# Hybrid decoder layer, first attention: values as the stationary operand in column halves, heads of a long and a short row tile in turn, transposes three units behind the scores

## The chip, the cores and the metric

The kernel runs on one core of a Trainium2 chip. A core has TensorE (PE; its weight loads, PEld, are recorded apart), VectorE (DVE), ScalarE (ACT), GpSimd (POOL) and SyncE (SP), which issues DMAs. Matrix products go to PSUM (eight banks of 128 partitions x 512 float32), everything else lives in SBUF. The metric is device time of one launch in microseconds (us), lower is better, as the median of several runs.

## What is computed

One layer on 512 tokens, width 1024. A combined projection feeds two causal attentions of eight heads each, whose gated outputs pass one output projection and a LayerNorm with a residual. The first attention (branch A) is the one that the change touches: each query attends to the 128 keys that an indexer ranks highest. Cut to what matters:

```python
h = x @ w_in[l]
(qa, ka, va, ga, iq, ik, iw, c_q, c_kv, k_rope, gb) = _split_cols(h)
# branch A, per block of 128 queries
score = jnp.einsum('bth,bths->bts', iwb, jax.nn.relu(logits))
_, sel = lax.top_k(score, k_top)
att = jnp.einsum('bthd,btkhd->bhtk', qb, ks) * scale
p = jax.nn.softmax(att, axis=-1)
o = jnp.einsum('bhtk,btkhd->bthd', p, vs)
o_a = _dsa_branch(qa, ka, va, iq, ik, iw) * jax.nn.silu(ga)
o_b = _mla_branch(...) * jax.nn.silu(gb)
out = jnp.concatenate([o_a, o_b], axis=-1) @ w_out[l]
x = _layernorm(DEEPNORM_ALPHA * x + out, ln_g[l], ln_b[l])
```

## The kernel before

Every engine has its own hand-written instruction list; semaphores join them. Up to 166 us the projections run, each product split into high and low parts (`products`, L1117), and beside them the indexer: its logits (`idx_logits`, L1221) use four groups of 32 array rows at once. VectorE finds the top keys and leaves a bias per query and key (`spans`), so that the selection becomes a mask over all keys up to the row.

The two attentions are one loop over **units** `u`, a head of a row tile of 128 queries: 0 to 31 are attention A (`NU_A` = 32), 32 to 63 attention B (`NU` = 64). `ORDER = [3, 2, 1, 0]` says which row tile comes first: heads of the tile with 512 keys, then 384, 256, 128. N is the number of keys of a unit. In step `u` of the loop the engines do:

- TensorE: `scores(u)` (A: L1308 and L1311, the high and low parts of queries and keys; B: L1318, float32) into one of two banks `ps_s`, free when the mask of u - 2 is done; `transposes(u - 2)` (L1353, `T_LAG` = 2), the N/128 tiles of the probabilities into one of two banks `ps_pT`, free when their copy is done; `outputs(u - 4)` (A: L1369, B: L1384, `PV_LAG` = 4). For A the stationary operand is a 128 x 128 tile of the transposed probabilities, streamed are the 64 columns of the head's values; the result has queries as partitions.
- VectorE: `mask_unit(u)` (L944) adds the mask into `probs` (four buffers) and takes the row maximum. For A, per row tile, `normalise` (L960, L961) and `apply_gate` (L970); for B `probs_low` (L975, the low part of the transposed probabilities), `read_pair` (L990) and others. In steps 3 to 6 it also does `qpe_blocks` (L932), a part of B's queries.
- ScalarE: `copy_probsT(u - 2)` (L704) from the bank to `probsT` (three buffers), then `exp_unit(u)` (L684), whose sum per row goes to `row_sum`; the high parts of B's values, `vb_high` (L728), at `VB_EARLY` = 20, 32 and 33.
- GpSimd: splits the output weights into high and low parts (L515, L519), then two of the four low parts of B's values (L522), then the second half of the weights' low parts (L528), then the merging of B's head pairs (L332) and the scaling of B's gate (`scale_gate`, L504).

The gated rows of A are turned by `o_transposes(i, 0)` (L1398): the first row tile at step `O_FIRST + T_LAG` = 18, the others during B. The products with the output weights, `out_products` (L1425), fill TensorE during B: the first half of the first row tile from step `A_HALF_AT` = 34, two matmuls a step, the rest from step 49.

## Time and profile before

| | |
|---|---|
| median of 3 runs | 301.89 us (301.46 to 301.92) |
| profiled execution | 301.67 us, span 299.9 us |
| TensorE busy | 291.2 us (97%) |
| TensorE weight loads | 248.6 us (83%) |
| VectorE busy | 228.5 us (76%) |
| ScalarE busy | 165.6 us (55%) |
| GpSimd busy | 169.8 us (57%) |
| first mask of A to first score of B | 166.4 to 208.0 us |
| granted TensorE clock | 1.00 of full speed (2.4 GHz) in every stretch up to 290 us |

Busy time is the union of an engine's recorded instructions. A record runs from an instruction's start to its end and overlaps with the next one's, so what an instruction costs an engine that is full is the distance from start to start; the chain of waits gives this directly. The difference of about 1.8 us between the execution's time and its span lies around the span.

### The profile page before, as it was taken

The numbers are of one execution on the slowest core, as the hardware profiler recorded it, in microseconds if no ns is written. First come the engines' busy times: TensorE is split into PE (matmuls) and PEld (weight loads), VectorE is DVE, ScalarE is ACT, GpSimd is POOL, SyncE is SP. The second block draws the span as 40 slices with busy tenths as digits, with TensorE's granted clock in tenths as the row PEclk, the third lists the DMA queues.
The fourth block names the chain that finished last, engine by engine and source line by source line (L and its number), as shares of the span: only waits on it lengthen the run. The fifth ranks groups of instructions, "written<-read, shape, count | busy, mean of one in ns | idle before, by whom it ended". The sixth has DMA issues, their size and how long they took to land.

```text
span 299.9 us, 5192 instructions
## 1 busy us (share of the span) xinstructions
PE 291.2 (97%) x1664; PEld 248.6 (83%) x1664; DVE 228.5 (76%) x523; ACT 165.6 (55%) x397; POOL 169.8 (57%) x197
## 2 busy tenths in 40 slices
PE   8999999999999999999999999999999999999990
PEld 7999987778888888888888789998677788888890
DVE  2898689879999999994134663564898878977785
ACT  4754533692252272383267787888877786553200
POOL 5798965106999975445317697630594161817211
PEclk9999999999999999999999999999999999999996
DMA  7965552200533723220056577301940000030412
GB/s 230 354 183 179 144 149 75 67 0 0 154 96 102 207 76 105 70 72 0 0 149 143 211 203 156 125 2 43 359 161 3 0 0 2 36 106 3 140 70 72
DMA packets 19547, 31.86 MB, mean 106 GB/s; under 512 B 6496, under 2 KB 9056, under 8 KB 19520
## 3 DMA queue, kind: packets, MB, share of 16 engines
q1 hardware_dynamic: 19088, 31.35, 34.4%
q8 instruction: 14, 0.23, 0.3%
q10 hardware_dynamic: 432, 0.18, 0.3%
q14 instruction: 13, 0.11, 0.1%
HBM read 26.28 MB, written 2.10 MB: 95 GB/s over the span
## 4 chain that ended last, share of the span: by engine, by line
PE 93%; DVE 2%; DMA 1%; ACT 1%; issue 1%; DVEq 0%; ACTq 0%
PE ps L1117 50%; PE ps L1425 15%; PE ps L1353 6%; PE ps L1318 5%; PE ps L1369 5%; PE ps L1384 3%; PE ps L1308 2%; PE ps L1132 2%; PE ps L1311 2%; PE ps L1221 1%; DMA w_raw<-in_w_in 1%; PE ps L1242 1%; PE ps L1398 1%; DVE y_last L1031 0%; ACT probs L684 0%
## 5 line engine op out<-in xcount | busy, mean ns | idle before, releaser
L474 POOL TENSOR_TENSOR w_lo<-w_raw,w_hi 128x512 fp32r<-128x512 f32 (+3 forms) x62 | 79.3, 1301 | 34.0 <-ACT w_hi L573 33.8
L1117 PE MATMUL ps<-w_hi,x_lo 128*128 128x512 f32 (+2 forms) x224 | 82.6, 372 | 0.0
L1117 PE MATMUL ps<-w_lo,x_hi 128*128 128x512 f32 (+2 forms) x224 | 82.5, 371 | 0.0
L573 ACT ACTIVATE w_hi<-w_raw 128x512 fp32r<-128x512 f32 (+3 forms) x62 | 35.9, 590 | 68.9 <-PE ps L1117 61.8
L1117 PE MATMUL ps<-w_hi,x_hi 128*128 128x512 f32 (+1 forms) x188 | 73.6, 391 | 0.0
L1117 PEld LDWEIGHTS ps<-w_hi,x_lo 128*128 128x128 f32 x224 | 42.1, 188 | 6.5
L1117 PEld LDWEIGHTS ps<-w_lo,x_hi 128*128 128x128 f32 x224 | 42.2, 188 | 6.0
L1425 PE MATMUL ps<-wo_hi,oT 128*128 128x512 f32 (+1 forms) x144 | 43.5, 372 | 0.0
L1117 PEld LDWEIGHTS ps<-w_hi,x_hi 128*128 128x128 f32 x188 | 35.3, 188 | 7.1 <-ACT w_hi L573 0.7
L684 ACT ACTIVATE probs<-probs,small 128x512 f32<-128x512 f32 (+3 forms) x64 | 35.8, 559 | 7.6 <-DVE small L944 7.0
L1353 PE MATMUL ps<-ident,probs 128*128 128x128 f32 x160 | 28.3, 274 | 0.4 <-ACT probs L684 0.2
L1425 PEld LDWEIGHTS ps<-wo_hi,oT 128*128 128x128 f32 x144 | 25.7, 189 | 3.3
L1353 PEld LDWEIGHTS ps<-ident,probs 128*128 128x128 f32 x160 | 20.1, 140 | 9.5 <-issue 5.2
L332 POOL TENSOR_TENSOR obT<-half_sum,crossed 64x128 f32<-64x128 f32 x30 | 15.7, 522 | 17.8 <-ACT crossed L737 16.1
L901 DVE MATCH_REPLACE8 score<-small,score 128x256 f32<-128x256 f32 (+2 forms) x48 | 25.7, 554 | 0.0
L944 DVE CUSTOM_DVE_ANT_0 probs<-ps,score 128x512 f32<-128x512 f32 (+2 forms) x24 | 13.3, 556 | 15.1 <-PE ps L1311 15.1
L898 DVE MAX8 small<-score 128x8 f32<-128x256 f32 (+2 forms) x48 | 23.7, 556 | 0.0
L944 DVE CUSTOM_DVE_ANT_0 probs<-ps,causal 128x128 f32<-128x128 f32 (+3 forms) x40 | 17.8, 444 | 7.0 <-PE ps L1318 3.4
L1318 PE MATMUL ps<-kbT,qbT 96*128 96x512 f32 (+3 forms) x64 | 22.7, 435 | 0.0
L1369 PE MATMUL ps<-va,probsT 128*128 128x64 f32 x160 | 21.4, 264 | 0.0
L1369 PEld LDWEIGHTS ps<-va,probsT 128*128 128x128 f32 x160 | 20.5, 193 | 0.6 <-issue 0.6
L975 DVE TENSOR_TENSOR probsT_b<-ps,probsT_b 128x512 fp32r<-128x512 f32 (+3 forms) x32 | 15.6, 488 | 5.0 <-ACT probsT_b L704 4.7
(164 smaller groups left out, 548.5 us busy)
## 6 DMA issues: line engine op xcount, KB each, us to landing
w_raw<-in_w_in SPq DMA_DIRECT2D x20, 512.0 KB, 3.7
...
```

Of the source, the lines that this page charges most:

```text
L332: eng.tensor_tensor(obT[rows, g % 4], half_sum[rows, g % 2, a], crossed[rows, g % 2], ALU.add).then_inc(pair_merged, 1)
L474: pool.tensor_tensor(w_lo[:, s, 0:n], w_raw[:, s, 0:n], w_hi[:, s, 0:n], ALU.subtract).then_inc(w_lo_ready, 1)
L573: act.activation(dst, w_raw[:, s, 0:n], ACT.Copy).then_inc(w_hi_ready, 1)
L684: act.activation(probs[:, u % NPROBS, 0:N], probs[:, u % NPROBS, 0:N], ACT.Exp, bias=neg_max[:, u % 8:u % 8 + 1], scale=-1.0, accum_out=ro ...
L898: step(V.max(top8[:, 8 * j:8 * j + 8], sc))
L901: step(V.match_replace(out=sc, in_to_replace=top8[:, 8 * j:8 * j + 8], in_values=sc, imm_value=TAKEN))
L944: V.tensor_tensor_reduce(out=probs[:, u % NPROBS, 0:N], in0=ps_s[:, u % 2, 0:N], in1=bias, scale=-scale, scalar=3.0e38, op0=ALU.add, op1=A ...
L1117: ins = mm(dst, a, b, start=start and j == 0, stop=stop and j == len(pairs) - 1)
L1318: ins = mm(ps_s[:, b, 0:N], qbT[:, h, t], kbT[:, h, 0:N], start=True, stop=True)
L1353: ins = nc.tensor.transpose(bank[:, j * P:(j + 1) * P], probs[:, u % NPROBS, j * P:(j + 1) * P], ident[:, :])
L1369: ins = mm(ps_o[:, v % 2, h * A_DIM:(h + 1) * A_DIM], probsT[:, u % 3, j * P:(j + 1) * P], va[:, j, h * A_DIM:(h + 1) * A_DIM], start=(j = ...
L1425: ins = mm(out_ps(i, b), oT[i % 2][:, o, k, :], w[:, wcols], start=first, stop=final)
```

## The change

Attention A's loop is written anew; B's arithmetic stays.

- **Order.** Units 0 to 15 take heads of the tiles with 512 and 128 keys in turn, units 16 to 31 those of 384 and 256 (`BLOCKS`). `row_sum` has its columns by rank (`sum_col`).
- **Lags.** Transposes of A come three steps behind the scores (`A_T_LAG`), outputs five (`A_PV_LAG`), for four units at once (`u % 4 == 3`).
- **Outputs** (new L1465). The head's 64 value columns are stationary, 128 columns of the transposed probabilities stream. Of two heads of one row tile the first writes partitions 0 to 63, the second 64 to 127 of the same bank columns, and their matmuls alternate. The result is already turned (head dimension as partitions). Each of the four row tiles has its own bank (`oa_bank`), two of them the banks of the output products.
- **Copies.** VectorE copies three of four transposed units of A, ScalarE the fourth (`by_dve`, `ACT_COPY`), into nine buffers (`buffer_of`, `copy_free`).
- **Gate.** Division and gate move: `row_sums_a` (reciprocals on VectorE, after all units of a block), `scale_gate_a` (GpSimd multiplies the gate's rows), `o_transposes(v, 0)` turns the scaled gate instead of the gated rows, at steps 28, 36, 38, 30 (`TURN_AT`), `turn_gate` (ScalarE) copies it to SBUF, `gate_oaT` (VectorE) multiplies it with the outputs, a step later. `copy_oT_hi` and `oT_low` read the product there; for the first row tile the latter is on GpSimd.
- **Around it.** `VB_EARLY` is 22, the first half of the output products starts at step 41 with three matmuls a step, and GpSimd does its last two weight splits between its first merges.

The diff, cut to its core:

```diff
+    BLOCKS = [(0, 3), (1, 2)]
+    A_RANK = [v for block in BLOCKS for v in block]
+    BLOCK_UNITS = 2 * HEADS
     def unit(u):
-        v, h = divmod(u, HEADS)
+        if u < NU_A:
+            n, r = divmod(u, BLOCK_UNITS)
+            v, h = BLOCKS[n][r % 2], r // 2
+        else:
+            v, h = divmod(u, HEADS)
         m = ORDER[v % TT]
         return v, m, h, (m + 1) * P
 
-    O_AFTER = [[NU_A + HEADS * (i + 1) + OT_AT - T_LAG + b for b in range(2)] for i in range(TT - 1)] + [[NU, NU]]
-    O_AFTER[0][0] = O_FIRST
+    def turned_at(u):
+        return [w for w in (u - A_T_LAG, u - T_LAG) if 0 <= w < NU and (w < NU_A) == (w == u - A_T_LAG)]
+    def buffer_of(u):
+        r = u % BLOCK_UNITS % 7
+        return r if r < 5 else r + 2 * (u // BLOCK_UNITS)
+    def last_user(u):
+        return max([w for w in range(u) if buffer_of(w) == buffer_of(u)], default=None)
+    def sum_col(u):
+        v, m, h, N = unit(u)
+        return HEADS * (A_RANK.index(v) if v < TT else v) + h
+    O_AFTER = [[turned_at(TURN_AT[i])[-1], NU_A + HEADS * (i + 1) + OT_AT - T_LAG + 1 if i < TT - 1 else NU] for i in range(TT)]
...
-    probsT = sb("probsT", 26, [P, 3, BANK])
+    probsT = [sb(f"probsT{j}", kib, [P, BANK]) for j, kib in enumerate((24, 26, 28, 30, 92, 88, 90, 94, 96))]
...
+        def by_dve(u):
+            return u < NU_A and u % 4 != ACT_COPY
+        def wait_copied(eng, u):
+            n = sum(by_dve(w) for w in range(u + 1))
+            if by_dve(u):
+                eng.wait_ge(probsT_copied_dve, n)
+            else:
+                eng.wait_ge(probsT_copied, u + 1 - n)
+        def copy_free(eng, u):
+            if u < NU_A:
+                if last_user(u) is not None:
+                    eng.wait_ge(pv_done, 4 * (last_user(u) // 4 + 1))
+                elif buffer_of(u) >= 7:
+                    eng.wait_ge(qpe_placed, 16 * P // SQ)
+                return probsT[buffer_of(u)][:, 0:unit(u)[3]]
+            if u >= NU_A + 3:
+                eng.wait_ge(pv_done, u - 2)
+            return probsT_b[:, u % 3, 0, 0:unit(u)[3]]
+        def oaT(i):
+            return gate[:, ORDER[i], 0:A_WIDTH].rearrange("p (a b) -> p a b", a=4)
+        def oa_bank(v):
+            return (ps_o, ps_y)[A_RANK.index(v) // 2][:, A_RANK.index(v) % 2]
...
-            for j in (3, 2):
+            def scale_gate_a(v):
+                m = ORDER[v]
+                pool.wait_ge(rinv_a_ready, A_RANK.index(v) // 2 + 1)
+                wait_tok(pool, G_GA, m)
+                g3 = gate[:, m, 0:A_WIDTH].rearrange("p (h d) -> p h d", h=HEADS)
+                r = rinv_a[:, HEADS * (A_RANK.index(v) % 2):HEADS * (A_RANK.index(v) % 2 + 1)]
+                pool.tensor_tensor(g3, g3, r.unsqueeze(2).broadcast_to([P, HEADS, A_DIM]), ALU.mult).then_inc(gate_a_scaled, 1)
+            def vb_low_pool(j):
                 pool.wait_ge(vb_hi_ready, VB_ORDER.index(j) + 1)
                 pool.tensor_tensor(vb_parts[j][:, :, 1:3], vb[:, j, :].rearrange("p (q a d) -> p q a d", a=2, d=V_DIM),
                                    vb_parts[j][:, :, 0:4:3], ALU.subtract).then_inc(vb_lo_pool, 1)
-            for j in range(KT, 2 * KT):
-                k = j // 2
+            def wo_low_b(k):
                 pool.wait_ge(raw_b_loaded[k - KT // 2], 16)
                 pool.wait_ge(wo_hi_ready, 2 * WO_ORDER.index(k) + 2)
-                pool.tensor_tensor(wo_lo(k, j % 2), wo_raw_b[:, k - KT // 2, j % 2], wo_hi[:, k, j % 2],
-                                   ALU.subtract).then_inc(w_lo_ready, 1)
+                for h in range(2):
+                    pool.tensor_tensor(wo_lo(k, h), wo_raw_b[:, k - KT // 2, h], wo_hi[:, k, h],
+                                       ALU.subtract).then_inc(w_lo_ready, 1)
+            for v in BLOCKS[0]:
+                scale_gate_a(v)
+            vb_low_pool(3)
+            oT_low(pool, 0, 0)
+            vb_low_pool(2)
+            for v in BLOCKS[1]:
+                scale_gate_a(v)
+            for k in range(KT // 2, KT - 2):
+                wo_low_b(k)
...
+                if g <= 2:
+                    wo_low_b(KT - 3 + g)
...
-                if u >= 3:
-                    act.wait_ge(pv_done, u - 2)
-                dst = probsT[:, u % 3, 0:N] if u < NU_A else probsT_b[:, u % 3, 0, 0:N]
+                dst = copy_free(act, u)
...
+            def turn_gate(v):
+                n = slot_of[v, 0]
+                act.wait_ge(transposed, n + 1)
+                act.activation(gate[:, ORDER[v], 0:A_WIDTH], ps_pT[:, n % 2], ACT.Copy).then_inc(gate_a_turned, 1)
...
+                if n == 0:
+                    act.wait_ge(pv_done, BLOCK_UNITS)
...
-            def normalise(v):
-                dve.wait_ge(pv_done, HEADS * (v + 1))
-                after(V.reciprocal(rinv, row_sum[:, HEADS * v:HEADS * (v + 1)]))
-                V.tensor_tensor(o_norm[:, :].rearrange("p (h d) -> p h d", h=HEADS),
-                                ps_o[:, v % 2].rearrange("p (h d) -> p h d", h=HEADS),
-                                rinv.unsqueeze(2).broadcast_to([P, HEADS, A_DIM]), ALU.mult).then_inc(o_ps_read, 1)
-            def apply_gate(v):
-                m = ORDER[v % TT]
-                cols = slice(A_WIDTH * (v // TT), A_WIDTH * (v // TT + 1))
-                dve.wait_ge(o_ps_read, v + 1)
-                wait_tok(dve, G_GA, m)
-                V.tensor_tensor(gate[:, m, cols], o_norm[:, :], gate[:, m, cols], ALU.mult).then_inc(o_ready, 1)
+            def copy_probsT(u):
+                dve.wait_ge(transposed, slot_of[u] + 1)
+                V.tensor_copy(copy_free(dve, u), ps_pT[:, slot_of[u] % 2, 0:unit(u)[3]]).then_inc(probsT_copied_dve, 1)
+            def row_sums_a(n):
+                dve.wait_ge(probs_ready, BLOCK_UNITS * (n + 1))
+                if n > 0:
+                    dve.wait_ge(gate_a_scaled, 2 * n)
+                V.reciprocal(rinv_a, row_sum[:, BLOCK_UNITS * n:BLOCK_UNITS * (n + 1)]).then_inc(rinv_a_ready, 1)
+            def gate_oaT(v):
+                half = gate[:, ORDER[v], 0:A_WIDTH]
+                dve.wait_ge(gate_a_turned, A_RANK.index(v) + 1)
+                dve.wait_ge(pv_done, BLOCK_UNITS * (A_RANK.index(v) // 2 + 1))
+                V.tensor_tensor(half, oa_bank(v), half, ALU.mult).then_inc(o_ps_read, 1)
...
-                if 0 < v <= TT and j == PV_LAG and v != TT - 1:
-                    normalise(v - 1)
-                if 0 < v <= TT and j == PV_LAG + 1 and v != TT - 1:
-                    apply_gate(v - 1)
-                if u == NU_A:
-                    normalise(TT - 2)
-                if u == NU_A + 2:
-                    apply_gate(TT - 2)
+                if u in (BLOCK_UNITS + 2, NU_A + 2):
+                    row_sums_a(u // BLOCK_UNITS - 1)
+                if u - 1 in TURN_AT:
+                    gate_oaT(TURN_AT.index(u - 1))
                 if v > TT and j == 2:
                     row_sums(v - 1)
                 if PET_AT <= u < PET_AT + TT:
                     qpe_blocks(u - PET_AT)
-                if u == O_FIRST + T_LAG + 1:
-                    oT_low(V, 0, 0)
...
-                    if h == 0:
-                        if v < 2:
-                            pe.wait_ge(acc_read[v], ACC_LAST[v])
-                        else:
-                            pe.wait_ge(o_ps_read, v - 1)
-                        if v == 0:
-                            for t in range(TT):
-                                wait_tok(pe, G_V, t)
-                    pe.wait_ge(probsT_copied, u + 1)
-                    for j in range(m + 1):
-                        ins = mm(ps_o[:, v % 2, h * A_DIM:(h + 1) * A_DIM], probsT[:, u % 3, j * P:(j + 1) * P],
-                                 va[:, j, h * A_DIM:(h + 1) * A_DIM], start=(j == 0), stop=(j == m))
-                    ins.then_inc(pv_done, 1)
+                    if u % 4 < 3:
+                        return
+                    if u % BLOCK_UNITS == 3:
+                        for b in range(2):
+                            bank = 2 * (u // BLOCK_UNITS) + b
+                            pe.wait_ge(acc_read[bank], ACC_LAST[bank])
+                        for t in range(TT):
+                            wait_tok(pe, G_V, t)
+                    for w in (u - 3, u - 2):
+                        v, m, h, N = unit(w)
+                        for a in range(2):
+                            wait_copied(pe, w + 2 * a)
+                        for j in range(m + 1):
+                            for a in range(2):
+                                ins = mm(oa_bank(v)[A_DIM * a:A_DIM * (a + 1), h // 2 * P:(h // 2 + 1) * P],
+                                         va[:, j, (h + a) * A_DIM:(h + a + 1) * A_DIM],
+                                         probsT[buffer_of(w + 2 * a)][:, j * P:(j + 1) * P], start=(j == 0), stop=(j == m))
+                                if j == m:
+                                    ins.then_inc(pv_done, 1)
...
-                            pe.wait_ge(acc_read[2 + b], ACC_LAST[2 + b])
+                            pe.wait_ge(o_ps_read, 3 + b)
...
-                if 0 <= u - T_LAG < NU:
-                    transposes(u - T_LAG)
-                if u - PV_LAG >= 0:
+                for w in turned_at(u):
+                    transposes(w)
+                if 0 <= u - A_PV_LAG < NU_A:
+                    outputs(u - A_PV_LAG)
+                if u - PV_LAG >= NU_A:
                     outputs(u - PV_LAG)
                 i, j = divmod(u - NU_A, HEADS)
-                if u == O_FIRST + T_LAG:
-                    o_transposes(0, 0)
-                if 0 < i < TT and OT_AT <= j < OT_AT + 2 and (i > 1 or j > OT_AT):
-                    o_transposes(i - 1, j - OT_AT)
-                if 0 <= u - A_HALF_AT < 12:
-                    out_products(0, 2 * (u - A_HALF_AT), 2 * (u - A_HALF_AT + 1))
+                for t in range(TT):
+                    if u == TURN_AT[t]:
+                        o_transposes(t, 0)
+                if 0 < i < TT and j == OT_AT + 1:
+                    o_transposes(i - 1, 1)
+                if 0 <= u - A_HALF_AT < 8:
+                    out_products(0, 3 * (u - A_HALF_AT), 3 * (u - A_HALF_AT + 1))
...
-O_FIRST = 16
-A_HALF_AT = 34
+O_FIRST = 33
+TURN_AT = [28, 36, 38, 30]
+A_T_LAG, A_PV_LAG = 3, 5
+ACT_COPY = 3
+VB_EARLY = 22
+A_HALF_AT = 41
```

TensorE, steady stretch of attention A. Before, the heads of the 512-key tile; L1308 and L1311 are scores, L1353 transposes, L1369 outputs:

```order
L1308 MATMUL ps<-kaT,qaT 128x512
L1311 MATMUL ps<-kaT_swap,qaT 128x512
L1353 MATMUL ps<-ident,probs 128x128 x4
L1369 MATMUL ps<-va,probsT 128x64 x4
L1308 MATMUL ps<-kaT,qaT 128x512
```

After, one step with outputs and its neighbours; L1399 and L1402 are the scores, L1444 the transposes, L1465 the outputs (the numbers in probsT_105 and so on tell the nine buffers apart):

```order
L1399 MATMUL ps<-kaT,qaT 128x512
L1402 MATMUL ps<-kaT_swap,qaT 128x512
L1444 MATMUL ps<-ident,probs 128x128
L1465 MATMUL ps<-probsT_105,va 64x128
L1465 MATMUL ps<-probsT_107,va 64x128
...
L1465 MATMUL ps<-probsT_106,va 64x128
L1465 MATMUL ps<-probsT_101,va 64x128
L1399 MATMUL ps<-kaT,qaT 128x128
L1402 MATMUL ps<-kaT_swap,qaT 128x128
L1444 MATMUL ps<-ident,probs 128x128 x4
```

The four output matmuls that stood in every step now stand as ten (three more pairs of the first two are left out) in every fourth, with streamed and stationary operand exchanged, and a long score is followed by a short transpose.

VectorE, steps 19 and 20 of attention A, with the semaphores that each row waits for. Before, masks (L944) and little else:

```order
L944 ISA probs,small<-ps,score 128x256 [waits transposed,scores_ready]
L944 ISA small 128x1
L342 TENSOR_TENSOR oT_68<-ps,oT_68 128x512 [waits oT_hi_ready]
L944 ISA probs,small<-ps,score 128x256 [waits transposed,scores_ready]
L944 ISA small 128x1
```

After, from mask 19 on (L1034) with the copies (L1049) of units 16 and 17:

```order
L1034 ISA probs,small<-ps,score 128x256 [waits transposed,scores_ready]
L1034 ISA small 128x1
L1049 COPY probsT_101<-ps 128x384 [waits pv_done,transposed]
L1034 ISA probs,small<-ps,score 128x384 [waits transposed,scores_ready]
L1034 ISA small 128x1
L1049 COPY probsT_102<-ps 128x256 [waits pv_done,transposed]
```

A copy now stands between most masks, and it waits for outputs (`pv_done`) as well as for its transposes.

TensorE, first steps of attention B (L1318, new L1409, are its scores). Before, at step 35, the output products (L1425) fill each step:

```order
L1318 MATMUL ps<-kbT,qbT 128x512
L1353 MATMUL ps<-ident,probs 128x128 x4
L1369 MATMUL ps<-va,probsT 128x64
L1425 MATMUL ps<-wo_hi,oT_68 128x512
L1425 MATMUL ps<-wo_lo_a,oT_68 128x512
```

After, steps 33 to 36:

```order
L1409 MATMUL ps<-kbT,qbT 128x512
L1444 MATMUL ps<-ident,probs 128x128 x3
L1409 MATMUL ps<-kbT,qbT 128x512
L1444 MATMUL ps<-ident,probs 128x128 x6
L1409 MATMUL ps<-kbT,qbT 128x512
L1444 MATMUL ps<-ident,probs 128x128 x4
```

The products are gone from these steps and come from step 41 on.

## Rows read from the trace of the kernel before

**Rows 1.** The page: busy time and share by engine; the chain of waits by engine.

```profile
PE 291.2 (97%) x1664; PEld 248.6 (83%) x1664; DVE 228.5 (76%) x523; ACT 165.6 (55%) x397; POOL 169.8 (57%) x197
...
PE 93%; DVE 2%; DMA 1%; ACT 1%; issue 1%; DVEq 0%; ACTq 0%
```

**Rows 2.** Windows: stretch, length, busy us (records) of PE, PEld, DVE, ACT, POOL, clock.

```profile
172.20:208.00 35.80, 35.56 (x296) 33.83 (x294) 19.22 (x71) 29.72 (x92) 21.01 (x25) 1.00 0.38 102
```

**Rows 3.** The chain of waits in attention A: start, length, what.

```profile
177.01 0.84 PE ps L1369 x8
177.85 0.29 PE ps L1308
178.13 0.23 PE ps L1311
178.37 0.44 PE ps L1353 x4
```

**Rows 4.** Waits, 165 to 240 us: us in total, times, longest.

```profile
DVE probs L944 <- PE ps L1311: 18.4, 25, 2.5
```

**Rows 5.** A's output matmuls: ns min/median/max, first and last start.

```profile
L1369 PE MATMUL ps<-va,probsT x160: 219/275/275, 175.1 to 213.8; 128*128 128x64 f32 x160
```

**Rows 6.** The chain: scores of B with 128 streamed float32 columns.

```profile
254.12 0.22 PE ps L1318 x2
```

**Rows 7.** Timeline of PE around the indexer's logits: start, length, line, shapes, count.

```profile
48.47 0.39 PE L1117 MATMUL ps<-w_hi,x_lo 128*128 128x512 f32 x1
48.79 0.45 PE L1221 MATMUL ps<-ik_hi,iq_hi 32*128 32x384 f32 x4
49.07 0.35 PE L1221 MATMUL ps<-ik_lo,iq_hi 32*128 32x384 f32 x4
49.24 0.35 PE L1221 MATMUL ps<-ik_hi,iq_lo 32*128 32x384 f32 x4
49.52 0.50 PE L1117 MATMUL ps<-w_hi,x_hi 128*128 128x512 f32 x1
49.85 0.39 PE L1117 MATMUL ps<-w_lo,x_hi 128*128 128x512 f32 x1
```

**Rows 8.** The chain: scores behind transposes; two products with output weights.

```profile
173.11 0.23 PE ps L1308
...
212.06 0.52 PE ps L1425 x2
```

**Rows 9.** Timeline of DVE: masks, copies, a small transpose [idle before <-releaser].

```profile
167.01 0.69 DVE L944 CUSTOM_DVE_ANT_0 probs<-ps,score 128x512 f32<-128x512 f32 x1
167.62 0.08 DVE L944 DVE_READ_ACCUMULATOR2_ANT small<- 128x1 f32 x1
167.74 2.52 DVE L952 COPY kbT<-ps 64x512 f32<-64x512 f32 x4
...
174.22 0.44 DVE L932 STREAM_TRANSPOSE qpe_blk<-qpe_tok 128x256 f32<-128x256 f32 x1
174.59 0.65 DVE L944 CUSTOM_DVE_ANT_0 probs<-ps,score 128x512 f32<-128x512 f32 x1
...
202.72 0.29 DVE L944 CUSTOM_DVE_ANT_0 probs<-ps,causal 128x128 f32<-128x128 f32 x1 [0.45 <-PE ps L1311]
202.94 0.08 DVE L944 DVE_READ_ACCUMULATOR2_ANT small<- 128x1 f32 x1
```

**Rows 10.** Timeline of ACT: a copy and an exponential of 512 columns.

```profile
174.34 0.59 ACT L704 ACTIVATE probsT<-ps 128x512 f32<-128x512 f32 x1
174.82 0.72 ACT L684 ACTIVATE probs<-probs,small 128x512 f32<-128x512 f32 x1
...
175.53 0.59 ACT L704 ACTIVATE probsT<-ps 128x512 f32<-128x512 f32 x1
```

**Rows 11.** Timeline of POOL: last weight split; a gate's scaling.

```profile
193.71 2.51 POOL L519 TENSOR_TENSOR wo_lo_a<-w_raw,wo_hi 128x512 fp32r<-128x512 f32 x2
...
230.01 1.05 POOL L504 TENSOR_TENSOR gate<-gate,small 128x512 f32<-128x512 f32 x1 [0.88 <-POOL obT L332]
```

42 lines of the change are left out of this document (23 added, 19 removed).

## The prediction

> **What bounds the kernel now.** I read the busy shares and the chain of waits first: TensorE is busy for 97% of the span and stands for 93% of the chain [rows 1]. Then the stretches: in the first attention (172.2 to 208) TensorE is busy 35.56 of 35.80 us while VectorE is busy 19.22 and ScalarE 29.72 [rows 2]. So what counts is TensorE's work in a row, unless the change makes it wait. Next, what one unit (a head of a row tile) costs there: pieces of the chain are start to start, so they add up. A long unit (512 keys) takes 0.29 + 0.23 us for its two score matmuls, 0.44 for four transposes and 0.84 for probabilities times values: eight recorded matmuls, two for each of four key chunks [rows 3]. So a chunk costs 0.21 us, though only 64 columns stream. The last part is the largest of the unit, and VectorE waits for it in the end: 18.4 us of its idle time before the masks is waiting for scores [rows 4].
>
> **Values stationary.** All 160 recorded matmuls of this step [rows 5] change form. In the old form each loads 128 stationary columns and streams 64. In the new one each loads 64 and streams 128, and two heads' matmuls write different halves of the output partitions, in alternation. Two bounds. If the halves run one after the other, a chunk costs what a float32 matmul with 128 streamed columns costs here: 0.22 us for the pair of records [rows 6], no gain on 0.21. If they run side by side, two heads' chunks take that time together, 0.105 to 0.11 each: 80 chunks x 0.105 = 8.4 us saved. Which of the two? The nearest row is the indexer, with four row groups: twelve matmuls of 384 columns stand in three groups of four with one start each, 0.17 us from the second group to the third, which is the time of one such matmul [rows 7]. TensorE thus runs disjoint parts of the array side by side, by rows; by columns no row shows it, nor for float32. I take side by side, -8.4, and keep 0 as the other end.
>
> The Trainium skill, TensorEngine Tiling (Array Packing), section Key Properties, says that different tiles load and multiply in parallel and that changing the tiling mode drains the engine. By its first half the gain is the -8.4 just given; its second half speaks against this change, and by it the eight groups of outputs below must pay something. The indexer's row agrees with both halves, for row tiles.
>
> **Changes of array form.** The outputs now come in eight groups of four units, each entered from and left to full-array matmuls. The indexer's excursion has the same price tag: the last full matmul starts at 48.47 and streams 0.23; the first one after it starts at 49.52 and is followed only 0.33 later instead of 0.23. That is 0.82 + 0.10 us, of which 3 x 0.17 is work: 0.41 over [rows 7]. It contains the exposed first load of four tiles. The least is none, if the halves switch freely. I take 0.35, nearer to the row: 8 x 0.35 = +2.8 (0 to 3.3).
>
> **Scores behind transposes.** A long score pair costs 0.52 right behind an output step but its first matmul only 0.23 behind transposes [rows 3, 8]. Before, nearly every unit stood behind outputs; now one in four. About ten long units gain 0.06: -0.6.
>
> **VectorE copies three of four transposed tiles.** Its own pace, start to start: mask of 512 columns 0.61, copy of 512 columns 0.61 (four in 2.52), mask of 128 columns 0.22 [rows 9]. I price the copy of 128 at 0.22 too. A pair (long and short) costs VectorE 0.61 + 0.22 for masks, 0.61 for the long copy and 0.11 for half the short ones: 1.55 us. TensorE needs for the pair 0.46 + 0.23 for scores, 0.55 for transposes, 5 x 0.105 for outputs and 0.18 for the switch: 1.95. ScalarE has two exponentials, 0.71 for the one of 512 columns and less for the one of 128, and a short copy every second pair, where even a 512-wide one costs it 0.48 [rows 10]: at most 1.7. So in the steady stretch TensorE still bounds, with VectorE at 80%; it would have to lose 0.4 us per pair before it takes over.
>
> At the start there is no such cover. Outputs begin only at unit step 8 (before: 4), and score 8 needs mask 6. Until then VectorE has masks 2 to 6 (3 x 0.61 + 2 x 0.22), copies 0 to 2 (1.44) and three of its four small transposes for the queries at 0.37 [rows 9]: 4.8 us, starting half a us behind TensorE. TensorE has scores 2 to 7 and transposes 0 to 4: 2.07 + 1.54 = 3.6 us. It waits 5.3 - 3.6 = about +1.8 (0.8 to 2.3).
>
> **Added waits.** First, the copy of unit 16 (VectorE, step 19) goes into a buffer last read by unit 14, whose outputs TensorE issues only in step 20. Behind that copy stand mask 20 and copy 17; transposes 18 need the bank that copy 16 frees, scores 22 need mask 20. After the outputs TensorE has only 0.23 us of scores before it meets the 0.48 of the copy, then again at mask 20: +0.5 (0.2 to 1.0). Second, at steps 33 to 35 VectorE has the two low parts of the values (512 columns, 0.61 each like the copy) between copy 30 and mask 34; ScalarE's third high part waits for them, and its copies of 31 and 32 queue behind that: TensorE waits about +0.5 for a bank (0 to 1.5). This stretch used to be covered by products with the output weights (0.52 the pair in [rows 8]); these now start at step 41 instead of 34. The 24 of them are the same work, so their move costs only what it uncovers.
>
> **Gates.** The gate's half is turned by TensorE four times, as the attended rows were before: 4 x 0.44 in both. Division and gating drop two 512-wide VectorE operations per row tile to one; VectorE isn't the bound, so 0. The scaling goes to GpSimd (four at 1.05), behind its weight splits, which end at 193.71 + 2.51 = 196.2 [rows 11]. TensorE turns the first gate at step 28. By the prices above the outputs of step 8 end at about 172.2 + 7.5, and each four steps after them take 3.9: step 28 ends near 199.5; GpSimd has the gate at 196.2 + 1.05 = 197.3. No cost, with 2 us of slack. No queue of DMAs is reordered; the later loads of the output weights still wait for the scores of unit 31, which come no later.
>
> **Sum** against the profiled execution's 301.67 us (span 299.9; the median of the runs is 301.89): -8.4 + 2.8 - 0.6 + 1.8 + 0.5 + 0.5 = -3.4. That is 298.3 on that execution and 298.5 on the median.
>
> **Rivals.** (a) The column halves do not run side by side. For it: no row shows column halves, and in this kernel a float32 matmul is two passes on the same tile in a row, which leaves only the second pass of one head to meet the first of the other. Against it: the indexer's groups. Then 0 replaces -8.4, and VectorE's lateness at the start remains: +2.8 + 1.8 + 0.5 - 0.6 (the waits at 16 partly vanish), 306.4. The gain is used up once a chunk costs 0.105 + 3.4 / 80 = 0.15 us; above that the kernel is slower than before. (b) The halves overlap, but VectorE sets the pace: its copies and masks queue for scores and banks so that each pair costs 0.2 more, 16 x 0.2 = +3.2, 301.7, no change. For it: VectorE would be at 80%, and its masks have slack of just two score banks. Against it: a copy needs no answer from TensorE before the next mask. (c) The switches are nearly free and waits are short: -8.4 + 0.5 - 0.6 + 1.8 + 0.5 = -6.2, 295.7. For it: the exposed part of the indexer's excursion belongs to four loads of 128 columns, here it would be two of 64. (d) The gate or the values' low parts come late from GpSimd at steps 28 to 36: +1.5 on the forecast, 300.0.
>
> **How the numbers follow.** Forecast 0.50, (c) 0.13, (d) 0.07: faster, 0.70. (b) 0.10: half of it within 0.2%, since a measurement of this kernel can tell about 0.2% (0.6 us) from no change; the rest splits evenly. (a) 0.20: slower. That makes faster 0.71, same 0.06, slower 0.23. The likeliest case alone, with the ends of its terms, runs from 296.0 to 301.0. The range for 8 in 10 adds most of (c) and all of (b) and (d), and of (a) the part in which the switches or waits are cheap: 295.0 to 304.5.
>
> **What would show it.** Right: in the new profile the output matmuls (128 streamed, 64 stationary columns) stand in the chain at about 0.42 us per group of eight records, 1.05 us for a group of four units; VectorE busy rises to nearly 30 us in the stretch of the first attention; TensorE has a gap of 1 to 2 us in its first 6 us, and another near the 20th unit; the first score of the second attention comes about 4 us earlier than 207.97. Wrong: eight records at 0.84 or more (a); a chain that runs through VectorE's copies in the steady stretch (b); full matmuls right behind the outputs without a delay (c); the gate's transposes waiting for GpSimd (d).

## The result and the profile after

| | before | changed |
|---|---|---|
| median, first set of runs | 301.92 us (301.46 to 302.25) | 300.47 us (299.97 to 300.50) |
| ratio to before, 95% interval | | 0.9947 [0.9932, 0.9963] |
| ratio in the repeat below | | 0.9953 [0.9935, 0.9971] |
| profiled execution | 301.67 us, span 299.9 | 300.80 us, span 299.0 |

The kernel is 1.5 us faster; the forecast was 3.4. One of the five executions of the first set, the profiled one, took 411.42 us at a granted TensorE clock of 0.658: range and ratio leave it out (the other four have a median of 300.37), and the rows of after come from a repeat of the unaltered kernel (first experiment), at a clock of 0.996.

The page, and windows over the changed stretch; the columns are those of [rows 1] and [rows 2]:

```profile
PE 288.9 (97%) x1664; PEld 240.4 (80%) x1664; DVE 233.3 (78%) x540; ACT 158.7 (53%) x377; POOL 174.0 (58%) x202
...
PE 93%; DVE 3%; issue 1%; ACT 1%; DVEq 0%; POOL 0%; POOLq 0%
```

```profile
172.17:206.90 34.73, 33.26 (x287) 25.33 (x285) 26.88 (x92) 22.77 (x73) 22.40 (x27) 1.00 0.45 124
```

TensorE's busy time falls by 2.3 us, its weight loads by 8.2, and VectorE's pieces of the chain add up to 10.3 us instead of 5.8. TensorE, which left 0.24 us of the stretch unused before [rows 2], now leaves 1.47. VectorE is busy 26.88 us of 34.73 there, 77% (the prediction expected nearly 30). The output matmuls answer to [rows 5], then one cycle of four units from the chain answers to [rows 3]:

```profile
L1465 PE MATMUL ps<-probsT,va x160: 272/273/324, 178.2 to 214.3; 128*64 128x128 f32 x160
```

```profile
182.62 1.24 PE ps L1465 x20
183.86 0.26 PE ps L1399
184.12 0.11 PE ps L1402
184.23 0.46 PE ps L1444 x4
184.69 0.23 PE ps L1399
184.92 0.23 PE ps L1402
...
185.47 0.66 PE ps L1444 x4
186.13 0.40 PE ps L1399
186.53 0.18 PE ps L1402
186.70 0.11 PE ps L1444
186.81 1.24 PE ps L1465 x20
```

Twenty records, the ten chunks of four units, take 1.24 us; the first score behind them takes 0.26, where it takes 0.12 behind outputs of the old form (below). That is 1.38 us a visit, and 1.40 was forecast. But the visits are 4.19 us apart where 3.9 was forecast: the second transposes take 0.66 instead of 0.44, the long score behind them 0.40 (0.45 a cycle before) instead of 0.23. Those extra pieces are waits inside TensorE's pieces, as the weight loads' own list of waits over the first attention shows (total us, times, longest):

```profile
PEld ps L1399 <- DVE small L1034: 2.6, 10, 0.5
...
PEld ps L1444 <- DVE probsT L1049: 1.6, 6, 0.5
```

### The profile page after: what moved, and what is told of

Same layout as the page of the kernel before. It is cut to its first block, busy times and chain, and to the rows that moved or that the text cites. A ratio compares the mean times of both kernels' runs of the same rounds, so it can differ in the third digit from the quotient of the medians.

```text
span 409.5 us, 5203 instructions
## 1 busy us (share of the span) xinstructions
PE 401.0 (98%) x1664; PEld 283.7 (69%) x1664; DVE 232.8 (57%) x540; ACT 163.0 (40%) x377; POOL 173.4 (42%) x202
## 4 chain that ended last, share of the span: by engine, by line
PE 97%; DVE 2%; issue 1%; DVEq 0%; POOL 0%; POOLq 0%
PE ps L1208 52%; PE ps L1523 15%; PE ps L1409 6%; PE ps L1444 6%; PE ps L1465 3%; PE ps L1482 3%; PE ps L1223 2%; PE ps L1399 2%; PE ps L1402 1%; PE ps L1496 1%; PE ps L1333 1%; PE ps L1312 1%; PE ps L1354 1%; PE ps L1321 0%; DVE probs L1034 0%
## 5 line engine op out<-in xcount | busy, mean ns | idle before, releaser
L1208 PE MATMUL ps<-w_hi,x_lo 128*128 128x512 f32 (+2 forms) x224 | 106.9, 478 | 0.0
L1208 PE MATMUL ps<-w_lo,x_hi 128*128 128x512 f32 (+2 forms) x224 | 106.8, 478 | 0.0
L1208 PE MATMUL ps<-w_hi,x_hi 128*128 128x512 f32 (+1 forms) x188 | 94.8, 504 | 0.0
L1523 PE MATMUL ps<-wo_hi,oT 128*128 128x512 f32 (+1 forms) x144 | 56.9, 473 | 0.0
L1444 PE MATMUL ps<-ident,probs 128*128 128x128 f32 x160 | 37.0, 345 | 0.4 <-DVE probsT L1049 0.3
L1523 PEld LDWEIGHTS ps<-wo_hi,oT 128*128 128x128 f32 x144 | 30.5, 223 | 8.9 <-issue 2.0
L1444 PEld LDWEIGHTS ps<-ident,probs 128*128 128x128 f32 x160 | 23.4, 157 | 16.9 <-issue 11.2
L1034 DVE CUSTOM_DVE_ANT_0 probs<-ps,causal 128x128 f32<-128x128 f32 (+3 forms) x40 | 17.8, 446 | 28.0 <-PE ps L1409 25.2
L1409 PE MATMUL ps<-kbT,qbT 96*128 96x512 f32 (+3 forms) x64 | 31.9, 588 | 0.0
L784 ACT ACTIVATE probsT_b<-ps 128x512 fp32r<-128x512 f32 (+3 forms) x32 | 14.0, 438 | 40.1 <-PE ps L1444 40.1
L1482 PE MATMUL ps<-probsT_b,vb_parts 128*128 128x256 f32 x80 | 22.2, 382 | 0.0
L1015 DVE TENSOR_TENSOR kaT<-ps,kaT 64x512 fp32r<-64x512 f32 x8 | 5.5, 689 | 28.5 <-ACT kaT L711 28.4
```

The source lines that it names most:

```text
L1034: V.tensor_tensor_reduce(out=probs[:, u % NPROBS, 0:N], in0=ps_s[:, u % 2, 0:N], in1=bias, scale=-scale, scalar=3.0e38, op0=ALU.add, op1=A ...
L1208: ins = mm(dst, a, b, start=start and j == 0, stop=stop and j == len(pairs) - 1)
L1409: ins = mm(ps_s[:, b, 0:N], qbT[:, h, t], kbT[:, h, 0:N], start=True, stop=True)
L1444: ins = nc.tensor.transpose(bank[:, j * P:(j + 1) * P], probs[:, u % NPROBS, j * P:(j + 1) * P], ident[:, :])
L1482: ins = mm(ps_o[:, g % 2, 2 * P * a:2 * P * (a + 1)], vb_parts[j][:, h // 2, 2 * a:2 * a + 2].rearrange("p a d -> p (a d)"), probsT_b[:, u ...
L1523: ins = mm(out_ps(i, b), oT[i % 2][:, o, k, :], w[:, wcols], start=first, stop=final)
```

## The experiments

All ratios are to the kernel before, measured in the same set of runs. Behind the first, edits are against the changed kernel.

A median of one kernel moves by some tenths of a microsecond from set to set, and most edits here are worth no more. The traces say why and help. Nothing ahead of the first attention was edited, yet in the profiled runs of the changed kernel and its variants its first score starts anywhere from 164.94 to 167.16 us. From there on they repeat: the first outputs come 12.36 to 12.40 us later wherever the edit doesn't touch that part, and from the sixth score of B to the end of the span it is 83.2 to 83.4 us in all of them. So the stretch between these two marks holds what an edit does. In us, from one profiled run of each kernel, by the chain:

| kernel | first score of A | from there to the sixth score of B | less the changed kernel |
|---|---|---|---|
| before | 165.63 | 51.18 | +1.36 |
| changed | 165.91 | 49.82 | |
| one head after the other | 165.40 | 52.80 | +2.98 |
| old form | 165.88 | 56.24 | +6.42 |
| two units a visit | 164.94 | 50.58 | +0.76 |
| ScalarE copies two of four | 165.65 | 47.67 | -2.15 |
| ScalarE copies the first four | 165.65 | 49.20 | -0.62 |
| buffers of the second block | 167.16 | 48.86 | -0.96 |
| turned gate ahead of the exponential | 165.73 | 49.50 | -0.32 |
| third high part later | 165.53 | 49.61 | -0.21 |
| gates cut short | 166.81 | 49.37 | -0.45 |
| low parts cut short | 165.58 | 49.32 | -0.50 |
| copy of attended rows later | 166.41 | 49.77 | -0.05 |
| three edits together | 166.06 | 46.63 | -3.19 |
| copies, buffers, rows later | 165.50 | 46.60 | -3.22 |
| the same, high part later too | 165.99 | 46.41 | -3.41 |

**The changed kernel again.** No edit.

> The changed kernel once more, for a profile at the full clock. Every theory: about 1.5 us faster than the kernel before. If the column halves run side by side, a step of outputs (20 records, ten chunks) takes 1.05 to 1.2 us in the chain; if not, 2.1.

300.74 us, 0.9953 [0.9935, 0.9971]. It repeats the result.

**Is the gain the column halves?** Two runs. The first takes the two heads' chunks one head after the other instead of in alternation:

```diff
-                        for j in range(m + 1):
-                            for a in range(2):
+                        for a in range(2):
+                            for j in range(m + 1):
```

> Of two heads first all chunks of the one, then all of the other; otherwise the changed kernel. If side by side was the gain, nothing meets any more and the 80 chunks cost 0.21 us again: 0.1 x 80 = 8 us slower than the changed kernel, less what TensorE then no longer waits (at most 3): +5 to +8. If the halves never met, no difference.

303.62 us, 1.0051 [1.0031, 1.0070]: 2.9 us over the changed kernel, less than expected. The chain shows why. The visits of the first block, then of the second:

```profile
182.59 1.73 PE ps L1465 x20
...
201.60 1.51 PE ps L1465 x20
```

Four visits are longer by 0.49 and four by 0.27: 3.0 us, the measured difference. But 1.73 is not serial either; fully serial would be 20 x 0.105 to 0.109 (next run). The starts of the single records show what happens. Within a head they stand 0.109 us apart, as they do in the changed kernel, where a record of the other half starts 0.007 behind each. Of the first head's eight records the last three start at 183.116, 183.225 and 183.334, but the next head's first one has started at 183.013. So TensorE starts matmuls of the free half ahead of those of the busy half that stand before them in the program, and lays four records of one head over the next.

The second run undoes the form alone. Order, lag, copies and waits stay; the heads no longer share the array, and what reads the attended values further on finds them in another arrangement than it expects:

```diff
-                                ins = mm(oa_bank(v)[A_DIM * a:A_DIM * (a + 1), h // 2 * P:(h // 2 + 1) * P],
-                                         va[:, j, (h + a) * A_DIM:(h + a + 1) * A_DIM],
-                                         probsT[buffer_of(w + 2 * a)][:, j * P:(j + 1) * P], start=(j == 0), stop=(j == m))
+                                ins = mm(oa_bank(v)[:, (h + a) * A_DIM:(h + a + 1) * A_DIM],
+                                         probsT[buffer_of(w + 2 * a)][:, j * P:(j + 1) * P],
+                                         va[:, j, (h + a) * A_DIM:(h + a + 1) * A_DIM], start=(j == 0), stop=(j == m))
```

> Undoes one part: the order of units, the lag, the copies and the waits of the changed kernel stay, but each chunk is again 128 stationary columns of probabilities with 64 columns of values streaming, one head after the other, so the attended values land in the old layout and what reads them further on gets them wrongly arranged. If the new form gives what I read in the trace, a group of 20 records takes 20 x 0.105 = 2.1 us instead of 1.24 + 0.15: 0.71 x 8 = 5.7 us more work on TensorE, of which the waits for VectorE in the first attention (2 to 3.5 us) swallow a part: 302.5 to 305 against 300.5. If the new form itself gives little and the order of units gave the gain, it stays within 0.6 of 300.5.

307.13 us, 1.0168 [1.0152, 1.0185]. This splits the change in two. The form gives 6.7 us (the difference of the ratios, 0.0221, of 302; 6.4 between the marks of the table), more than the 5.6 forecast for it. The order of units costs 5.2 us (307.13 against 301.91) where 2.2 was forecast. The chain of a cycle, and windows over a visit and over what stands between two visits; below them the same windows of the changed kernel (length, then busy us of PE, PEld, DVE, ACT, POOL):

```profile
183.36 2.18 PE ps L1465 x20
185.54 0.12 PE ps L1399
...
187.01 0.65 PE ps L1444 x4
187.67 0.39 PE ps L1399
```

```profile
183.36:185.54 2.18, 2.18 (x22) 2.18 (x21) 0.83 (x3) 1.16 (x4) 2.18 (x5) 1.00 0.14 18
185.54:188.34 2.80, 2.76 (x20) 2.27 (x20) 2.37 (x9) 1.52 (x6) 0.62 (x2) 1.00 0.92 262
```

```profile
182.62:183.86 1.24, 1.24 (x21) 1.07 (x21) 0.82 (x3) 0.92 (x3) 1.24 (x2) 1.00 0.45 76
183.86:186.81 2.95, 2.92 (x20) 2.21 (x22) 2.38 (x9) 1.76 (x8) 1.88 (x4) 1.00 0.66 155
```

A visit is 0.94 us longer in the old form, and yet the 0.65 and 0.39 behind it stand there as before: the stretch between visits shrinks by only 0.15, of which 0.14 is the first score behind the visit. The last column groups say it for VectorE: within a visit it is busy 0.83 us whether the visit lasts 1.24 or 2.18, then needs 2.4 between the visits. While TensorE makes outputs it makes no scores and no transposes, and with two banks of each VectorE has nothing to work ahead on. So the load on VectorE counts between the visits, 2.4 of 2.95, with the waits of one engine for the other's answer on top, and not over the whole cycle. How much of the 4.19 this load makes, a later run tells (less for VectorE).

**What does a visit cost?** Two units instead of four a visit, 16 visits instead of 8:

```diff
-                    if u % 4 < 3:
+                    if u % 4 < 2:
...
-                    if u % BLOCK_UNITS == 3:
+                    if u % BLOCK_UNITS == 2:
...
-                    for w in (u - 3, u - 2):
+                    for w in (u - 2,):
```

> The outputs of the long pair of heads come one step before those of the short pair, in 16 visits to the column halves instead of 8; otherwise the changed kernel. If a visit costs the predicted 0.35 us, 2.8 slower less what the smaller bursts give back (at most 1.2): +1.4 to +2.8. If visits are nearly free and the burst is what makes TensorE wait afterwards, 0.5 to 1.2 faster.

301.44 us, 0.9992 [0.9981, 1.0003]: 1.2 us over the changed kernel for eight visits more (0.8 between the marks). In the chain (a visit of the two long units, the pair of scores behind it, a visit of the two short ones):

```profile
180.63 1.02 PE ps L1465 x16
181.65 0.43 PE ps L1399
...
182.42 0.37 PE ps L1465 x4
182.79 0.26 PE ps L1399
```

1.02 + 0.37 is 0.15 over 1.24, and a long score takes 0.43 instead of 0.23: 0.35 a visit, the term of the sum. The 0.43 holds no wait for another engine: the weight loads' rows show 0.17 us without a cause ahead of this score. Of the 2.8 us for eight visits 0.8 to 1.2 show in the time. A likely reason, not tested apart: a longer burst is cut in two, and each half keeps VectorE idle for less.

**Less for VectorE.** It copies two of four transposed tiles instead of three:

```diff
-            return u < NU_A and u % 4 != ACT_COPY
+            return u < NU_A and u % 4 < 2
```

> ScalarE copies two of every four transposed units of attention A (the second long one too), VectorE the other two; otherwise the changed kernel. In the changed kernel four steps take 4.2 to 4.3 us against 3.9 of TensorE's work. If VectorE's masks and copies between two steps of outputs are what TensorE waits for, four steps fall to about 3.9: 1.0 to 2.0 faster over the seven groups. If ScalarE or the mere chain from engine to engine sets the 4.2, no difference within 0.3, or slower.

298.59 us, 0.9892 [0.9876, 0.9908], 1.8 us below the changed kernel. Windows over a visit and behind it:

```profile
181.66:182.90 1.24, 1.24 (x22) 1.07 (x21) 0.83 (x3) 0.92 (x3) 1.24 (x2) 1.00 1.04 176
182.90:185.71 2.81, 2.81 (x21) 2.22 (x22) 1.77 (x7) 2.13 (x9) 2.60 (x5) 1.00 0.32 54
```

VectorE needs 1.77 between the visits instead of 2.38, and the visits are 4.05 apart instead of 4.19. The first three cycles gain 0.5 of the 1.0 by which they exceeded the forecast; the other half stays, with TensorE's weight loads still waiting for copies and masks, and isn't divided further. The rest comes at the start (0.6), at unit 16 (0.1), at the gates (0.4) and in the handover (0.5; table below).

**The start.** The first four copies all on ScalarE:

```diff
-            return u < NU_A and u % 4 != ACT_COPY
+            return 3 < u < NU_A and u % 4 != ACT_COPY
```

> ScalarE copies units 0 to 3, VectorE starts with unit 4; otherwise the changed kernel. If VectorE's load holds TensorE up before the first outputs, its 4.8 us until mask 6 lose 1.44 us: 0.8 to 1.4 us faster than the changed kernel. If something else sets that start (ScalarE, or waits from engine to engine), no difference within 0.3, or slower.

299.72 us, 0.9922 [0.9904, 0.9940], 1.0 us below by the medians. In the trace the first outputs start 11.80 us behind the first score instead of 12.40, and those 0.6 us stay (-0.62 between the marks); what the median shows above that lies outside the edited stretch. The chain of the start now runs through ScalarE's exponentials and copies.

**Unit 16.** The second block takes its buffers in another order, so that its first two copies go into buffers that nobody has read yet:

```diff
-        return r if r < 5 else r + 2 * (u // BLOCK_UNITS)
+        return r if u < BLOCK_UNITS else (7, 8, 2, 3, 4, 0, 1)[r]
```

> The copies of units 16 and 17 go to two buffers that nobody has read yet, so they do not wait for the outputs of units 12 to 15; otherwise the changed kernel. The predicted wait at step 20 was 0.5 us: 0.3 to 0.7 faster than the changed kernel. If that wait is hidden, no difference within 0.2.

299.74 us, 0.9916 [0.9896, 0.9937], 1.0 us below; the fourth and fifth visits are 3.99 us apart (192.26, 196.25) instead of 4.93, and -0.96 between the marks.

**The gates and the handover.** Two visits stand far apart in the changed kernel: 5.79 us over steps 28 to 32, where the gates are turned, and 7.66 over steps 33 to 36, the handover to the second attention. Five edits on the changed kernel looked for the cause. ScalarE turns the gate ahead of the exponential instead of behind it:

```diff
+                if u in TURN_AT:
+                    turn_gate(TURN_AT.index(u))
                 if 2 <= u < NU:
                     exp_unit(u)
...
-                if u in TURN_AT:
-                    turn_gate(TURN_AT.index(u))
```

> ScalarE copies the turned gate before the exponential of the same step instead of behind it; otherwise the changed kernel. If TensorE's transposes at steps 31 and 32 wait for the bank that this copy frees, it gives 0.5 to 1.0 us. If the wait there comes from the exponentials or masks, no difference or up to 0.5 slower.

300.34 us, 0.9955 [0.9941, 0.9970]: no difference in the medians, 0.3 us in the trace (the seventh visit comes 5.52 behind the sixth instead of 5.79). The third high part of B's values a step later:

```diff
-                if u == NU_A + 1:
+                if u == NU_A + 2:
                     vb_high(3)
```

> ScalarE's fourth high part of the values comes one step later, behind the copies of units 31 and 32 that TensorE waits for; otherwise the changed kernel. If this order costs what the trace shows at step 34 (TensorE waits 0.6 us for that copy), 0.3 to 0.8 faster. If GpSimd, which then gets its low part later, becomes the wait at step 36, no difference or slower.

300.35 us, 0.9955 [0.9939, 0.9971]: no difference in the medians, 0.2 us in the trace. The eighth visit comes 6.94 behind the seventh instead of 7.65, but most of that is lost again just behind it. Three quarters of the gate multiplication left out, in the first two row tiles:

```diff
-                V.tensor_tensor(half, oa_bank(v), half, ALU.mult).then_inc(o_ps_read, 1)
+                n = P if TURN_AT[v] < NU_A else A_WIDTH
+                V.tensor_tensor(half[:, 0:n], oa_bank(v)[:, 0:n], half[:, 0:n], ALU.mult).then_inc(o_ps_read, 1)
```

> Leaves out: the gate multiplication of the first two row tiles on VectorE (steps 29 and 31) covers 128 of 512 columns, so three quarters of those attended values go on ungated. All waits stay. It takes twice about 0.45 us off VectorE between its masks in steps 28 to 32. If VectorE's place in that stretch is what holds TensorE (my reading of the 5.8 us between the two groups of outputs there), and the stretch behind doesn't swallow it, the kernel is 0.5 to 0.9 us faster than the changed one: 299.7 to 300.1. If steps 32 to 36 swallow what arrives early, the group of outputs in step 32 comes 0.5 to 0.9 earlier in the trace and the time stays at 300.4 to 300.7.

300.45 us, 0.9943 [0.9929, 0.9958]: the medians don't part it from the changed kernel. The trace does: the seventh visit comes 5.39 behind the sixth instead of 5.79, and the sixth score of B has kept the gain (-0.45). So VectorE's gates hold TensorE for 0.4 us there. The end of that distance shows what else stands in it, the first score of B, with 0.86 (line numbers are one higher in this run):

```profile
205.07 0.86 PE ps L1410 x2
205.93 0.25 PE ps L1445 x2
206.18 1.24 PE ps L1466 x20
```

Three quarters of VectorE's two low parts left out, B's outputs reading another chunk's values in place of those two:

```diff
-                V.tensor_tensor(vb_parts[j][:, :, 1:3], vb[:, j, :].rearrange("p (q a d) -> p q a d", a=2, d=V_DIM),
-                                vb_parts[j][:, :, 0:4:3], ALU.subtract).then_inc(vb_lo_dve, 1)
+                V.tensor_tensor(vb_parts[j][:, 0:1, 1:3], vb[:, j, :].rearrange("p (q a d) -> p q a d", a=2, d=V_DIM)[:, 0:1],
+                                vb_parts[j][:, 0:1, 0:4:3], ALU.subtract).then_inc(vb_lo_dve, 1)
...
-                             vb_parts[j][:, h // 2, 2 * a:2 * a + 2].rearrange("p a d -> p (a d)"),
+                             vb_parts[j if j > 1 else 3][:, h // 2, 2 * a:2 * a + 2].rearrange("p a d -> p (a d)"),
```

> Leaves out: VectorE's two low parts of the values (step 33) cover 128 of 512 columns, and the outputs of the second attention read another chunk's values in place of those two. All waits and all other operations stay. It takes twice about 0.45 us off VectorE in the handover, where its work for steps 32 to 35 (four masks, two copies, two low parts, two subtractions, 5.5 to 6 us) is more than TensorE's. If VectorE's load there is what TensorE waits for, the kernel is 0.6 to 1.0 us faster than the changed one, 299.6 to 300.0. If the wait is for ScalarE or for the scores' two banks alone, it stays at 300.4 to 300.7.

300.21 us, 0.9940 [0.9927, 0.9953], 0.2 to 0.4 below the changed kernel, which the intervals hardly part. In the trace the handover takes 7.20 us instead of 7.66, and the marks keep it (-0.50). ScalarE's copy of the first attended rows three steps later, GpSimd's part of it behind the gates:

```diff
-            oT_low(pool, 0, 0)
             vb_low_pool(2)
             for v in BLOCKS[1]:
                 scale_gate_a(v)
+            oT_low(pool, 0, 0)
...
-O_FIRST = 33
+O_FIRST = 36
```

> The same move of the copy of the first attended rows, alone on the changed kernel. There the chain of the handover ran through VectorE (mask, copy 30, two low parts) and only its end through ScalarE. If one engine after the other is late by nearly the same, it brings nothing or little: 300.3 to 300.7; if ScalarE was the bound all along, 300.0 to 300.2.

301.07 us, 0.9964 [0.9953, 0.9975]: not faster. The medians say 0.3 slower, but the intervals overlap, and between the marks nothing changed (-0.05): in that profiled run the first attention merely began 0.5 later. The chain of the changed kernel in the handover:

```profile
208.76 0.47 DVE probsT L1049
209.23 1.21 DVE vb_parts L1075 x2
...
210.49 0.51 issue
211.00 0.37 ACT probsT L784
...
211.42 0.66 PE ps L1444 x4
```

Behind a mask stand the copy of unit 30 and the two low parts on VectorE, then ScalarE's third high part (the 0.51 of "issue" lies inside it), then its copy of unit 31, which frees the bank. An edit to one of the two engines finds the other nearly as late. Of the five edits four gained 0.2 to 0.5 us in the trace, and the fifth moved a copy that isn't in this chain at all.

**Three edits together.** The copies (two of four, the first four on ScalarE) and the buffers:

```diff
-        return r if r < 5 else r + 2 * (u // BLOCK_UNITS)
+        return r if u < BLOCK_UNITS else (7, 8, 2, 3, 4, 0, 1)[r]
...
-            return u < NU_A and u % 4 != ACT_COPY
+            return 3 < u < NU_A and u % 4 < 2
```

> Three edits of the runs before in one kernel: VectorE copies two of four transposed tiles, the first four copies all go to ScalarE, and the second block takes its buffers in another order, so that its first copy doesn't wait for outputs. Apart they gave 1.75, 1.0 and 1.0 us on the changed kernel's 300.5 to 300.7. If the waits lie one behind the other on the path (each was time in which TensorE stood), the gains add up in the main: 297.0 to 297.7. If they are the same slack taken back three times, because a stretch behind them swallows what arrives early, it comes out near the best of them alone, 298.2 to 298.6.

298.27 us, 0.9876 [0.9861, 0.9892], near the best of them alone by the medians. Between the marks it is -3.19, and there the gains add up once the start is counted once: both edits of the copies shorten it to the same 11.8 us from first score to first outputs, so to the -2.15 of two of four copies only unit 16 adds its -1.0. From the first score of B to the fifth it takes 7.0 us (202.05 to 209.04), and the chain there now runs through ScalarE:

```profile
204.83 1.04 ACT vb_parts L815 x2
...
207.03 0.41 ACT oT L797
...
207.45 0.61 ACT vb_parts L815
```

**ScalarE unloaded there.** Copies two of four, the buffers, and the move of the copy of the first attended rows (all three diffs as above):

> On the changed kernel: VectorE copies two of four tiles, the second block has its buffers in the other order, and what is new: ScalarE's copy of the first attended rows (0.6 us) moves from step 33 to step 36, and GpSimd takes its part of it behind the second block's gates instead of ahead of them. With three edits together (298.27) the chain of the handover ran through ScalarE: two high parts, this copy, the third high part, the last two copies. If ScalarE's queue is what TensorE waits for there, taking 0.4 us out of that chain shows in full: 297.6 to 297.9. If the scores' two banks and the masks stand right behind it, it stays at 298.2 to 298.5.

297.61 us, 0.9857 [0.9844, 0.9870], the lowest median of this study: 2.9 below the changed one, 4.3 below before. Against the run before it that is 0.6, as expected of an unloaded ScalarE, but the trace doesn't bear the reason out. From the first score of B to the fifth it still takes 6.98 us (201.47 to 208.45), between the marks 46.60 against 46.63, and the chain has only changed engines, to VectorE's two low parts:

```profile
205.60 1.22 DVE vb_parts L1075 x2
...
206.87 0.51 issue
207.38 0.38 ACT probsT L784
```

In this profiled run the first attention began 0.56 earlier (165.50 against 166.06). So the expected number came, and not for its reason. The same with the third high part a step later too:

> The first kernel of this call with one more move: ScalarE makes the third high part of the values (0.6 us) at step 34 instead of 33, behind the copies of units 31 and 32. Alone on the changed kernel that brought nothing. If ScalarE bounds the handover here, the copy of unit 31, for which TensorE waits, comes 0.6 us earlier: 0.3 to 0.6 below that kernel, 297.1 to 297.5. If the wait moves on to the masks, no difference.

297.64 us, 0.9855 [0.9839, 0.9871]: no further gain, although now the chain of the handover is TensorE's alone, 6.74 us instead of 7.18:

```profile
206.54 0.66 PE ps L1444 x6
207.19 0.86 PE ps L1409 x2
...
209.35 0.44 PE ps L1444 x4
```

Of its 0.44, 0.26 are lost just behind it, where the sixth score of B comes 2.61 behind the eighth visit instead of 2.35. That leaves 0.2, which these runs can't tell from nothing.

Distances between starts of the eight visits in the chain, in us:

| | first at | 1-2 | 2-3 | 3-4 | 4-5 | 5-6 | 6-7 | 7-8 |
|---|---|---|---|---|---|---|---|---|
| forecast | 178.3 | 3.9 | 3.9 | 3.9 | 4.4 | 3.9 | 5.3 | 7.2 |
| changed | 178.31 | 4.31 | 4.19 | 4.21 | 4.93 | 3.98 | 5.79 | 7.66 |
| old form | 178.26 | 5.10 | 4.98 | 5.00 | 5.83 | 4.77 | 6.59 | 8.44 |
| two of four copies | 177.49 | 4.17 | 4.05 | 3.97 | 4.79 | 3.92 | 5.38 | 7.21 |
| copies, buffers, rows later | 177.29 | 4.17 | 4.06 | 3.96 | 3.85 | 3.86 | 5.38 | 7.18 |

The forecast's last two distances are worked out now. 5.3 is a cycle of 3.9 and two turned gates of 0.44, with B's first score (0.86) in place of one of A's (0.35). 7.2 is a visit with its switch (1.40), four scores of B at 0.86, 17 transposes at 0.11 and the prediction's wait of 0.5. With two of four copies the chain doesn't pass the seventh visit; its place is taken from the records.

## Why the prediction was right or wrong

**The form (-8.4 and +2.8): right.** The halves run side by side, ten chunks in 1.24 us, and a visit with its switch costs 1.38 instead of 1.40. Undoing the form costs 6.7 where 5.6 was forecast; 0.6 of the difference is that a record of the old form took 0.109 us there (2.18 for 20), not 0.105. Rival (a) fell with its main claim. Its reason, that the two passes of one head stand in a row, didn't hold; even a whole head in a row keeps part of the overlap. Rival (c) fell too: the switch costs 0.35, as the trace of the doubled number of visits shows. The Trainium skill, TensorEngine Tiling (Array Packing), Key Properties, says both that tiles work in parallel and that a change of mode drains the engine; the trace agrees with the first, and for the second it has 0.35 us a visit.

**Scores behind transposes (-0.6): right in kind.** Long pairs take 0.46 where nothing is waited for.

**The start (+1.8): right.** First outputs at 178.31, forecast 178.3, and the chain there runs through VectorE's masks, a copy and its transposes for the queries. (The prediction's own terms give 5.3 - 3.6 = 1.7.) Taking VectorE's copies away there gave 0.6 back; then ScalarE bounds the start.

**Unit 16 (+0.5): right cause, too small.** The edit of the buffers gave 1.0 us, and the trace 0.94, inside the term's bounds of 0.2 to 1.0. The forecast set 0.23 us of scores against a copy of 0.48, then the mask behind it. In the trace TensorE stands idle for 0.33 us until the copy is done, and then loses 0.2 at nearly every piece, because VectorE has a mask, a copy, a mask and a copy in a row: three transposes take 0.55 instead of 0.33, the score behind them 0.37 instead of 0.18:

```profile
192.41 0.57 DVE probsT L1049
...
193.02 0.55 PE ps L1444 x3
193.57 0.37 PE ps L1399
```

**The steady stretch (0): wrong, and the first of two steps that failed.** The prediction set 1.55 us of VectorE against 1.95 of TensorE for a pair of units, found 80% and concluded that TensorE bounds. The 80% came true (77% over the whole stretch). But the outputs are gathered in visits, and in a visit TensorE gives VectorE nothing new. Between visits VectorE needs 2.4 of what should have been 2.5 (3.9 - 1.38), and each mask and copy starts only when TensorE's piece is done. The first three cycles took 0.4, 0.3 and 0.3 more than forecast, 1.0 in all. Taking a third of the copies off VectorE gave 0.5 of it back; the other 0.5 is put down to the same waits by the weight loads' rows, and no run takes it away alone. It is rival (b) in a milder form, whose own sentence "a copy needs no answer from TensorE before the next mask" missed that the mask does.

**Gates and handover (0 and +0.5): the second step that failed.** Gates were priced at nothing, "VectorE isn't the bound, so 0". Between the sixth and the seventh visit the chain runs mask, copy, VectorE's gate, mask, exponential, ScalarE's turned gate, and takes 5.79 us for 5.3:

```profile
202.85 0.11 DVE gate L1064
...
203.45 0.55 DVE probs L1034
...
204.04 0.71 ACT probs L766 x2
204.75 0.49 ACT gate L803
```

Shortening VectorE's gates brought the visit to 5.39, so nearly all of the 0.5 hangs on them: the step that failed is again that 80% of load was read as no wait. The handover took 7.66 for 7.2. There the products with the output weights stood before; they start at step 41 now, and the prediction priced one wait that they used to cover at 0.5, where about 1.0 came (6.74 with TensorE's work alone in the chain). No run puts the products back, so that they had covered it all is argued, not shown.

**The sum.** Waits over forecast: 1.0 + 0.1 + 0.5 + 0.5 + 0.5 = 2.6 us. Take the sixth score of B as the mark, at 216.81 before and 215.73 after. There the forecast stands at -3.9, since the changed kernel has 0.5 us more left to do (six products with output weights, 1.4, less two turned gates of 0.44). With the waits that is -1.3, and the trace has -1.1. From the mark to the end it is 83.1 us before and 83.3 after, 0.2 more and not 0.5; where the 0.3 go isn't traced. So the terms end at -0.8, and the profiled pair ends 0.9 apart, 301.67 and 300.80. The medians are 1.5 apart. The first score of A came 0.28 later in the profiled run of the changed kernel than in that of the kernel before; the rest is within what one pair of executions scatters (spans of the changed kernel reach from 298.2 to 299.1). That the time fell at all is no luck: the form was right, and its gain was larger than every wait together.

Two figures of the prediction don't follow from its terms. The ends of the likeliest case add up to 293.9 to 301.0, not 296.0 to 301.0. And its chances, with half of (b) as no change and the rest split evenly, make 0.725, 0.05 and 0.225, not 0.71, 0.06 and 0.23. Neither moves the forecast.

**The first score of B: right, and misleading.** It came at 204.06, 3.9 us earlier than 207.97, as forecast. Five units later only 1.1 were left. An early arrival at a stretch with waits of its own was counted as a gain.

**Rival (d): not seen.** GpSimd scales the gate in time and begins the first low part of the values at 196.83, more than 4 us ahead of the turned gate (201.17):

```profile
195.83 1.05 POOL L585 TENSOR_TENSOR gate<-gate,small 128x512 f32<-128x512 f32 x1
196.83 1.28 POOL L590 TENSOR_TENSOR vb_parts<-vb,vb_parts 128x512 fp32r<-128x512 f32 x1
```
